# The Hyena filter spectra of the first layer, made at other places of TensorE's queue in a hybrid four-branch backbone (one Trainium2 core)

## The reference

```python
def hyena_filter_spectra(length, w1, b1, freq, w2, b2, w3):
    t = jnp.linspace(0.0, 1.0, length, dtype=F32)[:, None]
    ...
    hdn = jnp.sin(freq[0].astype(F32) * (feats @ w1.astype(F32) + b1.astype(F32)))
    hdn = jnp.sin(freq[1].astype(F32) * (hdn @ w2.astype(F32) + b2.astype(F32)))
    h = (hdn @ w3.astype(F32)).reshape(length, HY_ORDER, 2, HY_W)
    ...
    h = h * jnp.exp(-t[:, :, None, None] * deltas)
    taps = jnp.concatenate([h[:, :, 0], jnp.zeros((1, HY_ORDER, HY_W), F32), h[:0:-1, :, 1]], axis=0)
    taps = taps / jnp.sum(jnp.abs(taps), axis=0, keepdims=True)
    return jnp.fft.rfft(taps, n=2 * length, axis=0)

# in each layer
h = rmsnorm(x, norm1[li]) * (1.0 + sc1) + sh1      # sc1, sh1 from silu(c) @ w_ada[li] + b_ada[li]
p = h @ w_in[li]
```

## Time and profile before

| | us |
|---|---|
| median of 3 runs | 1950.65 |
| lowest, highest | 1949.61, 1951.37 |
| profiled execution, whole | 1959.33 |
| profiled execution, from first to last instruction (span) | 1957.4 |
| TensorE busy | 1857.3 (95% of the span) |
| VectorE, ScalarE, GpSimd busy | 1289.3, 789.2, 609.3 |
| mean granted clock of TensorE | 0.977 |

### The profile page before, as it was taken

How to read it: one execution, slowest core, us unless ns; L and a number is a source line. 1 busy time by engine, 2 the same in 40 slices (tenths; PEclk the granted TensorE clock), 3 DMA queues, 4 the chain that set the end, 5 groups by cost and what they waited for, 6 DMA issues and landing times.

```text
span 1957.4 us, 31847 instructions
## 1 busy us (share of the span) xinstructions
PE 1857.3 (95%) x11070; PEld 1522.9 (78%) x11070; DVE 1289.3 (66%) x2122; ACT 789.2 (40%) x1627; POOL 609.3 (31%) x553
## 2 busy tenths in 40 slices
PE   6999899999999999999999999898899899989999
PEld 2556788767588888777888887687787689989999
DVE  4755867666856765358765776759686655567574
ACT  2325534356243233333322322356435544445453
POOL 3433244622312111163200223434455521143030
PEclk8999899999999999999999999999999999999999
DMA  7433111332234443334556556223214335554564
GB/s 235 131 106 108 44 45 54 86 123 81 80 130 151 139 155 114 97 130 160 183 172 197 174 197 194 80 76 86 77 44 137 101 112 180 173 162 151 183 183 140
DMA packets 210925, 252.98 MB, mean 129 GB/s; under 512 B 11715, under 2 KB 176900, under 8 KB 209796
## 3 DMA queue, kind: packets, MB, share of 16 engines
q1 hardware_dynamic: 207088, 235.01, 38.3%
q10 hardware_dynamic: 3732, 16.60, 2.3%
HBM read 245.29 MB, written 6.29 MB: 129 GB/s over the span
## 4 chain that ended last, share of the span: by engine, by line
PE 68%; DVE 13%; issue 10%; POOL 4%; ACT 3%; DMA 1%; ACTq 1%; DVEq 0%; POOLq 0%
PE psum L651 54%; PE psum L646 13%; DVE big L2551 3%; DVE rstd L2551 2%; DVE big L2560 1%; POOL whl L1525 1%; POOL big L3518 1%; PE psum L757 1%; ACT big L1764 1%; DVE big L2853 1%; POOL big L3386 1%; ACT big L1767 1%; ACT whl L1516 1%; DVE hhl L2720 1%; POOL big L1615 1%
## 5 line engine op out<-in xcount | busy, mean ns | idle before, releaser
L651 PE MATMUL psum<-hhl,whl 128*128 128x512 f32 (+1 forms) x4416 | 833.3, 347 | 24.5 <-DVE hhl L2720 15.0
L651 PEld LDWEIGHTS psum<-hhl,whl 128*128 128x128 f32 x4416 | 698.6, 192 | 149.3 <-issue 40.5
L1516 ACT CAST whl<-raw 128x512 fp32r<-128x512 f32 x656 | 374.2, 618 | 806.2 <-PE psum L651 801.2
L1525 DVE TENSOR_TENSOR whl<-raw,whl 128x512 fp32r<-128x512 f32 x480 | 333.7, 737 | 320.8 <-ACT whl L1516 319.9
L651 PE MATMUL psum<-bigr,whl 128*128 128x512 f32 (+1 forms) x2688 | 475.2, 337 | 5.0 <-DVEq L3295 2.5
L651 PEld LDWEIGHTS psum<-bigr,whl 128*128 128x128 f32 x2688 | 412.6, 190 | 61.1 <-issue 6.9
L1525 POOL TENSOR_TENSOR whl<-raw,whl 128x512 fp32r<-128x512 f32 x176 | 232.9, 1345 | 377.8 <-ACT whl L1516 359.4
L646 PE MATMUL psum<-big 128*128 128x128 f32 (+8 forms) x1572 | 249.1, 332 | 23.4 <-DMA big<-in_hy_w_dram 5.4
L646 PEld LDWEIGHTS psum<-big 128*128 128x128 f32 (+4 forms) x1572 | 168.5, 180 | 81.2 <-issue 50.2
L651 PE MATMUL psum<-whl,hhl 128*128 128x512 f32 x672 | 162.9, 401 | 10.6 <-POOL whl L1525 8.7
L3518 POOL TENSOR_TENSOR big<-big,tmp 128x512 f32<-128x512 f32 (+1 forms) x64 | 64.6, 1023 | 346.0 <-DVE tmp L3292 345.3
(11 more groups left out here) (185 smaller groups left out, 1483.7 us busy)
## 6 DMA issues: line engine op xcount, KB each, us to landing
raw<-in_w_mlp_dram SPq DMA_DIRECT2D x128, 512.0 KB, 3.8
raw<-in_w_in_dram SPq DMA_DIRECT2D x88, 512.0 KB, 3.7
big<-in_w_ada_dram SPq DMA_DIRECT2D x88, 512.0 KB, 5.1
raw<-in_w_gate_dram SPq DMA_DIRECT2D x64, 512.0 KB, 3.5
raw<-in_w_branch_dram SPq DMA_DIRECT2D x32, 512.0 KB, 3.5
raw<-in_w_ada_dram SPq DMA_DIRECT2D x24, 512.0 KB, 5.6
raw<-in_w_o_dram SPq DMA_DIRECT2D x16, 512.0 KB, 3.4
hy_spectra<-big ACTq DMA_DIRECT2D x2, 2560.0 KB, 9.3
```

Of the source, the lines that this page charges most:

```text
L651: m = nc.tensor.matmul(o_, a(p_), b(q_), start=first and i == 0, stop=last and i == 2, skip_group_check=shared)
L1516: nc.scalar.copy(whl[:, r, 0, ks], raw_of(n)[:, ks]).then_inc(S["hi_ready"], 1)
L1525: ins = eng.tensor_tensor(whl[:, r, 1, ks], raw_of(n)[:, ks], whl[:, r, 0, ks].bitcast(F32), ALU.subtract)
```

## The change

The second filter of the first layer is taken out of the start. Its taps now come after chunk 4 of the projection, its scale after chunk 8, its spectrum and Nyquist row after chunk 10. The filters of the second layer stay in the projection and are made in the slots that follow: taps after chunks 8 and 12, scale after 12 and 16, the rest after 14 and 18. The first filter's steps in the start stand later (taps after mod group 2, scale after group 6), its spectrum stands behind the norm's sums, where the second's was, and its Nyquist row after chunk 4. Every other engine is given the same order: VectorE's cut of (0, 0) after mod columns 1 and its reciprocal after mod columns 5, GpSimd makes the sums of (0, 1) in the projection instead of VectorE in the start, ScalarE's absolute values of (0, 0) come after `mod_row(5)`. ScalarE's square of the last slice of x is moved in front of the first splits of weights. No step is added or removed.

```diff
+        LATER = [(0, 1), (1, 0), (1, 1)]
...
                             turn(b, [stage[:, m, k * P:(k + 1) * P] for m in range(NT)]).then_inc(filled, 1)
+                    if g == 2:
                         filter_taps(0, 0)
-                    if g == 2:
-                        filter_taps(0, 1)
+                    if g == 4:
                         columns(1)
-                    if g == 4:
+                    if g == 6:
                         filter_scale(0, 0)
-                    if g == 6:
-                        filter_spectrum(0, 0)
-                        filter_nyquist(0, 0)
                 mod_turn(0, FIRST_MODS - 1)
-                filter_scale(0, 1)
...
                         if chunk == 4:
-                            filter_nyquist(0, 1)
-                        if chunk in (4, 12):
-                            filter_taps(1, chunk // 12)
-                        if chunk in (8, 16):
-                            filter_scale(1, chunk // 16)
-                        if chunk in (10, 18):
-                            filter_spectrum(1, chunk // 18)
-                            filter_nyquist(1, chunk // 18)
+                            filter_nyquist(0, 0)
+                        if chunk in (8, 12, 16):
+                            filter_scale(*LATER[chunk // 4 - 2])
+                        if chunk in (4, 8, 12):
+                            filter_taps(*LATER[chunk // 4 - 1])
+                        if chunk in (10, 14, 18):
+                            filter_spectrum(*LATER[(chunk - 10) // 4])
+                            filter_nyquist(*LATER[(chunk - 10) // 4])
...
                 if li == 0:
-                    filter_spectrum(0, 1)
+                    filter_spectrum(0, 0)
...
-                    if g in (2, 3):
-                        filter_taps(0, g - 2)
+                    if g == 5:
+                        filter_taps(0, 0)
...
+                last_square(0, slice(0, T))
                 for i in range(RING):
                     split_hi(act, split_strips[i])
...
-                    if g == 3:
+                    if g == 5:
                         filter_scale(0, 0)
-                    if g == 5:
-                        filter_spectrum(0, 0)
-                        filter_nyquist(0, 0)
                 amps(0, 0)
                 for i in range(RING):
                     split_lo(dve, split_strips[i])
-                filter_scale(0, 1)
```

More of the change, by code:

```diff
@@ L1827, in start_, with last_square @@
                             give_fill(act, ("x", k))
+                last_square(0, slice(0, T))
                 for i in range(RING):
                     split_hi(act, split_strips[i])
+            def last_square(n, tk):
+                act.wait_ge(S["sq_summed"], n + 1)
+                f(tmp[:, 0, tk], xT[:, KD - 1, tk], ACT.Square).then_inc(S["last_sq"], 1)
             def mod_row(li, g):
@@ L1856, in norm @@
                     act.wait_ge(S["x_added"], 24 * li + 8 * which)
-                act.wait_ge(S["sq_summed"], n + 1)
-                f(tmp[:, 0, tk], xT[:, KD - 1, tk], ACT.Square).then_inc(S["last_sq"], 1)
+                    last_square(n, tk)
                 if which:
@@ L2034, in dn @@
                     ahead(2)
-                    keep_spectra(0)
                     ahead(3)
                     gates()
-                    filter_taps(1, 0)
+                    filter_taps(0, 1)
                     silu(2)
@@ L2042, in dn @@
                     ahead(5)
+                    filter_taps(1, 0)
+                    keep_spectra(0)
                     silu(4)
@@ L2987, in dn @@
                     conv_block(1)
-                    filter_nyquist(0, 1)
-                    filter_cut(1, 0)
+                    filter_nyquist(0, 0)
+                    filter_cut(0, 1)
                     conv_block(2)
                     conv_block(3)
+                    filter_scale(0, 1)
+                    filter_cut(1, 0)
+                    conv_block(4)
+                    filter_spectrum(0, 1)
+                    filter_nyquist(0, 1)
+                    conv_block(5)
+                    gate_inputs()
                     filter_scale(1, 0)
-                    conv_block(4)
+                    filter_cut(1, 1)
+                    conv_block(6)
                     dve.wait_ge(spectra_kept, 16)
```

15 lines of the change are left out of this document (4 added, 11 removed).

## The result

| | before | after |
|---|---|---|
| median, us (4 runs each) | 1950.13 | 1962.05 |
| lowest, highest | 1949.60, 1951.37 | 1959.45, 1962.80 |
| ratio after/before | | 1.0048, interval 1.0029 to 1.0067 |

The change makes the kernel slower by 11.9 us on the medians (0.3 to 0.7% by the interval). The ratio of 1.0048 stands for less, 9.4 us; it agrees with the means if the profiled execution of before, 1959.33, is counted in. The forecast was +7.3 us, 1957.9, with 1952.7 to 1962.5 as its range. A second timing of both programs on another occasion gave 1.0062 (1.0044 to 1.008), +11.1 us on the medians. So the sign holds, and the range holds with 0.4 us to spare. The size is too small by about 4 us: where that lies is the subject here.

A forecast was written before the change was run, and what follows sets the result against it. The prediction took TensorE to bound the stretch before `amp` and the projection, GpSimd the norm. Its terms, −11.5 + 15.9 + 1.9 + 1.0, gave +7.3 us on 1950.65, so 1957.9, range 1952.7 to 1962.5.

The forecast's parts named there:

- the core of the forecast: Second filter's work: 3.6 us was free under the norm; after the change none is free, and the start's gain is capped.
- its 15.8 us: Start, before `amp`: TensorE work removed, 7.1 us for taps (0, 1) plus 8.7 for spectrum with Nyquist row.
- Part 1: Stretch before `amp`: `amp` at 56.0 instead of 67.46 us, a gain of 11.5, ends 9.3 and 14.1.
- rival (1): Start: clock returns some 10 us sooner, gain 13 to 14.1, net +2.3 to +3.9, no difference; chance 0.25.
- Part 2: Norm: TensorE idles some 6 us, the clock halves and the projection starts slow, +1.0 us, ends 0 and 3.
- Part 3: Projection: 15.9 us of second-filter work at full price plus net waits of 1.9 us, ends 0.5 and 3.
- (3): Scale and projection start: half clock holds through both, +9.6 to +12.6 us, 1960 to 1963; chance 0.15.
- (2): Projection: hidden slack hides more than 11 of 16 us, so faster, about 1942 us; chance 0.07.
- Its smaller way: Half-clock stretch 199.2 to 212.8 does not come, giving back 6.8 us at most and leaving +0.5.
- (4): Norm: spectrum (0, 0) is not hidden, which would need 8 us of error; given no own chance.

The follow-up runs named there:

- b_double: Kernel before, with the eight products of spectrum (1, 0) in the projection made twice: 1961.71 us, ratio 1.0040 to before.
- a_fill: Kernel after, with six of the eight products of spectrum (0, 0) made twice in the norm's idle time: 1960.76 us, ratio 1.0041 to before.
- h_two_back: Kernel after, with taps (0, 1) put back after mod group 3 and scale (0, 1) ahead of the norm's sums: 1953.24 us, ratio 0.9996 to before.
- b_thin: Kernel before, with taps (0, 1), spectrum (0, 0) and its Nyquist row cut to one 16-column product per bank: 1949.30 us, ratio 0.9987 to before.
- a_both: Kernel after, with taps ahead of the scale after chunks 8 and 12, and six spectrum (0, 0) products made twice: 1956.78 us, ratio 1.0016 to before.
- before again: Kernel before, unchanged, run for a second trace: 1953.12 us, ratio 1.0008 to before.
- after again: Kernel after, unchanged, run for a second trace: 1963.80 us, ratio 1.0062 to before.
- a_tapsfirst: Kernel after, with the next filter's taps ahead of the scale after chunks 8 and 12: 1956.76 us, ratio 1.0015 to before.
- b_wait: Kernel before, with taps (1, 1) directly behind scale (1, 0), after chunk 8 instead of chunk 12: 1954.82 us, ratio 1.0011 to before.

## Why the prediction came out right, and where it was too small

**What bounds the kernel.** Right for the projection and the norm, half right for the start. TensorE's work costs its full length in the projection (`b_double`) and nothing where TensorE waits for others (`a_fill`: 5.5 us free; `h_two_back`: 7.3 us put back for 1.1 us at `amp`, and the loss is gone). That was the core of the forecast. But the stretch before `amp` was called TensorE bound, and with 12.2 us of TensorE's work left out of it (`b_thin`) it gets only 3.4 to 4.5 us shorter. The prediction's gain came near the measured one because it followed the new order step by step, VectorE and the reads of weights included, and didn't just subtract its 15.8 us.

**Part 1, gain before `amp`: −11.5 forecast, −11.2 measured** (means of five and six executions). The steps were mostly there: reciprocal directly ahead of the last columns, TensorE waiting for weights (ahead of groups 4 and 6, 2.8 + 0.8 and 0.2 + 0.9 us, not ahead of 5 and 6), the scale at 46.05 where 46.4 was forecast. The clock was wrong: in the start of after 3.4 us are at half clock, in the five other executions with this start 6.8, and it is full again at 42.6 to 45.6, not at 49. All of the scale runs at full clock (3.70 us in all six), and `amp` comes at 54.0 to 55.8, 54.9 on the mean, and not at 56.0. That is the direction of rival (1), by less than it said. It was made good by a second error: `amp` of before is 66.1 on the mean and not 67.46. Two errors of 1.1 and 1.3 us cancelled, and that the gain was hit so closely is luck. The half clock of one profiled execution, which two of five have, had been taken for the kernel's own.

**Part 2, the norm.** Idle 5.95 us before the second slice (6 forecast), granted clock 0.50 there (the row of 883.24 in the earlier trace rows had it), second slice 13.5 us after `amp` (13.9 forecast), third 16.2 (16.6). `a_fill` shows that the idle time brings the half clock. The cost, 2.6 us at half clock inside the projection in after and 0.8 in its second execution, so 1.3 and 0.4 us, stands against 1.0 forecast. The rule of the Trainium skill that the prediction weighed ("TensorE: Matmul & The Clock Gate", section "HAM oscillation — how this bites in real kernels") held here: 5.95 us idle, granted clock 0.50 from 66.5 to 73.3.

**Part 3, the projection: +17.8 forecast, +21.9 measured** (131.1 and 132.05 against 109.7). This is the mis-sized term. Work and waits were right within 0.6 us: `a_both` measures the work at 15.4 us (15.9 forecast), ScalarE's wait of 0.66 in it, and 0.74 + 0.81 for banks and 0.24 for ScalarE bring it to 17.2. Missing is the half clock behind the bank waits: 6.8 us in both executions of after, at half speed 3.4 us. With the half clock that reached in from the norm (1.3 and 0.4) that makes 21.9 and 21.0, against 22.3 and 21.4 measured. The prediction had priced two waits of 0.6 to 0.8 us at their length, as "0.6 to 0.8 us each", and had put the risk of half clock only where 6 us are idle. The waits cost about three times their length. The Trainium skill ("TensorE: Matmul & The Clock Gate", section "A second HAM failure mode: psum-queue depth-cycling") tells of a matmul kernel that cycles through PSUM banks and idles for moments between groups of products, and whose clock swings between half and full. The half clock behind the bank waits of 0.74 and 0.81 us here agrees with it; that case is nearer to these waits than the one cited, and it was overlooked.

Against the forecast's +7.3: the projection takes 3.1 us more (the +1.0 of part 2 counted with it), the gain in the start is 0.3 smaller, and `amp` to third slice takes 0.3 less than in before. That gives +10.4, between the +9.0 and +11.9 of the two pairs of traces. The timings give +11.9 and +11.1 on the medians; their intervals hold it.

**Rivals.** (3) named this size, +9.6 to +12.6, but by half clock through the scale, which didn't come (that at the start of the projection did). (2) is excluded by `b_double`. Its smaller way, the half-clock stretch behind the projection, says nothing about the change either: it comes in all 14 traces, earlier or later (see below). (1) was right that the clock returns before the scale, but not in the gain nor in the net. (4): the spectrum is hidden, TensorE idles 5.95 us behind it.

**Open.** Why a wait of 0.8 us is followed by half clock 8 times in 11 wasn't settled. All eleven stand after the four products of a scale and three of the taps, which use 64 of the 128 rows. But that isn't what it takes. Right behind the projection, every trace has a bank wait of 1.10 us between products that use all 128 rows; this is the row of before, with which the half-clock stretch 199.2 to 212.8 of the earlier trace rows begins:

```profile
199.25 2.04 PE L646 MATMUL psum<-big 128*128 128x128 f32 x8 [1.10 <-DVEq L1494]
```

In 8 of the 14 traces half clock began from 0.2 us before the end of this wait to 0.7 us after it. In the other six (before again, after, after again, `a_both`, `a_tapsfirst`, `b_wait`) it came 11 to 13 us later. So this wait too is followed by it often and not always, at the same place of the same program. The waits of 0.8 to 1.4 us for slices of h ahead of the projection were not followed by it, in any trace; one of 2.2 us was, once in two.

## What to carry to other kernels

Before work is moved off an engine that waits, ask what it filled there: a scale of 3.6 us was free under the norm and taps of 3.7 under VectorE's sums; in a stretch where TensorE is the bound, these and the waits that they brought cost more than the start gained. Where two small steps share a ring of banks, put the one whose reader is slow (a reciprocal of 3.4 us) last: the same work in the other order took more than 5 us less. And a term that rests on a half-clock stretch of one profiled execution needs a second execution before it is believed.

## What the runs showed of the hardware

- Waits of 0.74 and 0.81 us between small products were followed by 3.4 or 6.8 us of granted clock 0.50 in 8 of 11 cases; 24 products then took 7.0 to 8.2 us instead of 5.75. A bank wait of 1.10 us behind the projection was followed by it in 8 of 14.
- A span of one and the same program (everything behind the projection, about 1755 us) had 51 to 72 us at half clock in different executions and ran from 1754 to 1764 us with it.
- An engine at half clock can be free of charge: 17.1 instead of 6.8 us of it in the start of before moved `amp` by 2.3 us, since TensorE otherwise waited 3.57 us for VectorE there.
